# One matmul for a weight block's products with the high and low parts of 256 tokens, in two halves of a PSUM bank

## The chip, the cores and the metric

The kernel runs on one core of one Trainium2 chip. A time is the device time of one execution in microseconds (us); the one given for a kernel is the median of its runs. Before the change that is 3179.44 us in three runs (3178.3 to 3180.76).

## What is computed

Two transformer blocks, each of two layers, follow each other on 256 tokens of 1024 channels, all in float32:

```python
# first block, for each of 2 layers
x = x + 0.5 * swiglu_ffn(rms_norm(x, ffn1_norm[i]), ffn1_w_in[i], ffn1_w_out[i])   # D_FF = 2816
proj = rms_norm(x, mix_norm[i]) @ w_in[i]
rx, rgate, q, k, v, f_logit, ga, gb = jnp.split(proj, split_idx, axis=-1)
ya = (rg_lru(causal_dwconv(rx, ...), ...) * jax.nn.gelu(rgate)) @ w_rnn_out[i]
yb = forgetting_attention(q, k, v, f_logit, ...) @ w_attn_out[i]                   # 8 heads of 128
merged = jax.nn.sigmoid(ga + mb_a) * ya + jax.nn.sigmoid(gb + mb_b) * yb
x = x + merged @ w_o[i]
x = x + 0.5 * swiglu_ffn(rms_norm(x, ffn2_norm[i]), ffn2_w_in[i], ffn2_w_out[i])
gate = jax.nn.sigmoid(rms_norm(x, ple_norm[i]) @ ple_w_gate[i] + ple_b_gate[i])
x = x + gate * (p[i] @ ple_w_proj[i])
# second block: x and a context of 256 tokens; layer 0 FFN, conformer convolution, FFN;
# layer 1 FFN, windowed attention with 16 query and 4 key heads, projection, FFN
```

## The kernel before, in words

**Products.** A float32 product is made of rounded parts: weight w = wh + wl, input x = xh + xl, and y = wh·xh + wh·xl + wl·xh. TensorE (PE) makes three matmuls of a block of 128 x 128 weights, on lines 683, 684 and 685 (962 to 964 in the values units, where the weights move and the input stands). The weights come as *units*: 1024 rows by 256 columns, 8 blocks deep (`kc`) and 2 tiles wide (`t`), so 16 products. The output units of the last third of an FFN are 6 deep: 12 products.

**Streaming.** A unit's raw weights come in by SP's DMAs, into 4 slots. ACT rounds them to `wh` (`hi`, line 1316, one instruction for each tile), DVE subtracts to get `wl` (`lo`, line 1787). Both do this for unit u + 2 while PE works on u: there are two buffers by parity. A unit's two tiles lie in two banks of PSUM, again by parity. Each engine's program is written out by hand, in order; semaphores link them: `mm_done` (a tile's products are there), `hi_done`, `lo_done`, `banks_free` (DVE or ACT has read the banks).

**Order of stages.** Layer of the first block, all at 256 tokens: FFN1, the mixer, FFN2, the PLE gate. An FFN goes in three groups: gate-and-up units (G), then four output units (O), whose result is added to x. The mixer goes through units for gates, the recurrence's input, queries and keys, then four *values units* (V0 to V3), four units of the merge gate (GB), four output units of the recurrence (RNN), four of the attention (ATT) and four of the output projection (WO). The heads are spread over them: from V3 on, step st does, between the two tiles of a unit and behind it, scores of head st (line 1000), turning head st - 1's probabilities (line 972) and its values. The second block mostly works on x and context together, 512 tokens at once; only its query units (K2_Q), output projection (K2_WO) and last FFN (K2_FFN4) are at 256.

**Norms that are put off.** Behind FFN1, the mixer and FFN2 of the first block, the next stage's first units work on x before its norm. For that, ACT and DVE do the following for each of the last four output units i. ACT: both `hi` of unit u + 2, squares of x (line 1352, `Tt`), x times the gain rounded (line 1360, `Fh` or `Hh`); for i = 3 a table load comes between the `hi`, and the squares stand ahead of the second. DVE: `lo` of tile 0, the low part of x for i - 1, the update of x (line 1967 through the helper on line 1779), `lo` of tile 1. PE sums the squares (line 723) ahead of block 4 of the next stage's first unit for the last, and spreads the roots (line 751) at block 7. `Fl` is the low part, `Rr` the roots.

**Readers of a unit's banks.** The x update is one instruction of 128 x 512 with factor 0.25; the values are copied by DVE (line 2202) to `Vb`; ACT takes the merge gate's tanh straight from the banks; RNN and ATT are multiplied by their gates in one instruction each; the queries of the second block are scaled by DVE (line 2523).

## Time and profile before

| what | value |
|---|---|
| median of three runs | 3179.44 us (3178.3 to 3180.76) |
| span of the profiled execution | 3176.8 us |
| PE busy | 3133.6 us, 99%, 21659 instructions |
| DVE busy | 2103.7 us, 66% |
| ACT busy | 1328.4 us, 42% |
| granted clock of PE | 9 tenths or more in each of the 40 slices |
| lines 683 to 685, x from `Fh`, `Fl` | 3296 products, 304 + 302 + 302 ns as the mean of one |

The profile is of one execution. Its span is 3176.8 us, about 2.6 us under the median of the runs, which holds what lies outside the span too. Matmuls overlap, so the mean duration of one is more than the time from one start to the next; the pitch is read from the timeline. A releaser in square brackets in a row is what ended the idle time before that instruction.

### The profile page before, as it was taken

To read this page: it belongs to the slowest core of one execution; us is meant where nothing else is said; L and a number is where in the kernel's file an instruction comes from. 1 tells how busy PE (TensorE), PEld (TensorE's weight loads), DVE (VectorE), ACT (ScalarE), POOL (GpSimd) and SP (SyncE) were. 2 spreads that over 40 slices of the span, in tenths; PEclk is the share of its full clock that TensorE was granted. 3 is DMA by queue.
4 is the path that set the end of the run, shared out by engine and by line. 5 is a ranking of instruction groups with operands and counts; after the bars stand their busy time and mean duration, and the time that the engine had idled before them with its cause. 6 is when DMAs were issued, how large, how long until landed. Compare 5 with 4: busy or idle time off the path is not lost.

```text
span 3176.8 us, 51940 instructions
## 1 busy us (share of the span) xinstructions
PE 3133.6 (99%) x21659; PEld 2775.9 (87%) x21659; DVE 2103.7 (66%) x3503; ACT 1328.4 (42%) x2009; POOL 2.3 (0%) x6
## 2 busy tenths in 40 slices
PE   8999999999999999999999999999999999999999
PEld 8999999999999999997888766788887888875999
DVE  6777756667677756657676487666646666464555
ACT  4455555455455554454232323422224222337444
POOL 0000000000000000000000000000000000000000
PEclk9999999999999999999999999999999999999999
DMA  7665446657655456665444454445435554340663
GB/s 207 186 172 175 152 137 181 181 185 205 183 172 171 139 161 175 179 224 147 146 133 139 134 145 135 141 125 159 133 108 148 154 147 124 116 146 1 188 184 107
DMA packets 682467, 488.05 MB, mean 154 GB/s; under 512 B 24575, under 2 KB 681337, under 8 KB 682233
## 3 DMA queue, kind: packets, MB, share of 16 engines
q1 hardware_dynamic: 677113, 480.21, 51.0%
q10 hardware_dynamic: 5120, 4.53, 0.6%
q8 instruction: 171, 2.80, 0.4%
q14 instruction: 63, 0.52, 0.1%
HBM read 474.57 MB, written 1.05 MB: 150 GB/s over the span
## 4 chain that ended last, share of the span: by engine, by line
PE 90%; DVE 4%; ACT 3%; DMA 1%; DVEq 1%; issue 1%; ACTq 0%; SPq 0%
PE ps L683 27%; PE ps L684 26%; PE ps L685 26%; DVE wl L1787 1%; PE ps L1144 1%; DVE Pp L1779 1%; PE ps L1269 1%; PE ps L1248 1%; ACT wh L1316 1%; DVE Hl L1779 1%; PE ps L1259 1%; PE ps L751 1%; PE ps L962 0%; PE ps L963 0%; PE ps L964 0%
## 5 line engine op out<-in xcount | busy, mean ns | idle before, releaser
L1787 DVE TENSOR_TENSOR wl<-raw,wh 128x1024 fp32r<-128x1024 f32 (+2 forms) x780 | 921.2, 1185 | 693.9 <-ACT wh L1316 692.0
L1316 ACT ACTIVATE wh<-raw 128x1024 fp32r<-128x1024 f32 (+2 forms) x780 | 794.1, 1026 | 1383.6 <-PE ps L685 1341.9
L683 PE MATMUL ps<-Fh,wh 128*128 128x256 f32 (+1 forms) x3296 | 1001.3, 304 | 6.3 <-DVE Fl L2458 3.0
L684 PE MATMUL ps<-Fl,wh 128*128 128x256 f32 (+1 forms) x3296 | 995.5, 302 | 0.0
L685 PE MATMUL ps<-Fh,wl 128*128 128x256 f32 (+1 forms) x3296 | 995.4, 302 | 0.0
L683 PE MATMUL ps<-Hh,wh 128*128 128x256 f32 (+1 forms) x2576 | 870.8, 338 | 6.9 <-DVE wl L1787 3.3
L684 PE MATMUL ps<-Hl,wh 128*128 128x256 f32 (+1 forms) x2576 | 856.6, 333 | 0.0
L685 PE MATMUL ps<-Hh,wl 128*128 128x256 f32 (+1 forms) x2576 | 856.4, 332 | 0.0
L683 PEld LDWEIGHTS ps<-Fh,wh 128*128 128x128 f32 x3296 | 629.7, 191 | 36.4 <-DVE Fl L2458 5.1
L685 PEld LDWEIGHTS ps<-Fh,wl 128*128 128x128 f32 x3296 | 629.8, 191 | 23.3
L684 PEld LDWEIGHTS ps<-Fl,wh 128*128 128x128 f32 x3296 | 629.9, 191 | 22.7
L683 PEld LDWEIGHTS ps<-Hh,wh 128*128 128x128 f32 x2576 | 488.7, 190 | 81.2 <-DVE Hl L1779 16.6
L685 PEld LDWEIGHTS ps<-Hh,wl 128*128 128x128 f32 x2576 | 488.9, 190 | 47.8
L684 PEld LDWEIGHTS ps<-Hl,wh 128*128 128x128 f32 x2576 | 489.0, 190 | 46.2 <-issue 1.0
L1779 DVE SCALAR_TENSOR_TENSOR QK<-raw,cs,QK 128x256 f32<-128x256 f32 x504 | 222.0, 482 | 17.9
L1445 ACT ACTIVATE Fh<-Pp 128x256 fp32r<-128x256 f32 (+1 forms) x176 | 85.9, 488 | 101.6 <-DVE Pp L1962 92.0
L1962 DVE TENSOR_TENSOR Pp<-Ss,ps 128x512 f32<-128x512 f32 (+1 forms) x88 | 54.7, 621 | 49.1 <-PE ps L685 43.9
L1779 DVE SCALAR_TENSOR_TENSOR Xx<-ps,G,Xx 128x256 f32<-128x256 f32 x112 | 52.3, 479 | 43.6 <-PE ps L685 41.2
L1932 DVE TENSOR_TENSOR Ss<-ps,Ss 128x256 f32<-128x256 f32 x88 | 37.4, 425 | 29.9 <-PE ps L685 20.9
L1405 ACT ACTIVATE Hh<-Pp,MOD 128x256 fp32r<-128x256 f32 x88 | 39.7, 501 | 40.1 <-DVE Pp L1779 40.1
L1983 DVE TENSOR_TENSOR Fl<-Pp,Fh 128x512 fp32r<-128x512 f32 (+1 forms) x88 | 54.4, 618 | 0.0
L1779 DVE SCALAR_TENSOR_TENSOR Ss<-Tt,ps 128x512 f32<-128x512 f32 (+1 forms) x88 | 54.1, 615 | 0.0
(307 smaller groups left out, 2204.8 us busy)
## 6 DMA issues: line engine op xcount, KB each, us to landing
raw<-in_ffn_w_in SPq DMA_DIRECT2D x176, 512.0 KB, 5.2
raw<-in_ffn_wi SPq DMA_DIRECT2D x176, 512.0 KB, 5.3
raw<-in_ada_w SPq DMA_DIRECT2D x144, 512.0 KB, 4.5
raw<-in_w_in SPq DMA_DIRECT2D x112, 512.0 KB, 4.6
raw<-in_ffn_w_out SPq DMA_DIRECT2D x64, 512.0 KB, 4.1
raw<-in_ffn_wo SPq DMA_DIRECT2D x64, 512.0 KB, 4.6
raw<-in_ffn_w_out SPq DMA_DIRECT2D x32, 384.0 KB, 3.8
raw<-in_ffn_wo SPq DMA_DIRECT2D x32, 384.0 KB, 3.8
```

Of the source, the lines that this page charges most:

```text
L683: nc.tensor.matmul(o, wh[:, u.par, kc, w], xh(kc), start=(kc == 0), stop=False)
L684: nc.tensor.matmul(o, wh[:, u.par, kc, w], xl(kc), start=False, stop=False)
L685: return nc.tensor.matmul(o, wl[:, u.par, kc, w], xh(kc), start=False, stop=(kc == kc_n - 1))
L751: mm = nc.tensor.matmul(ps[:, b, n // 4 * g:n // 4 * (g + 1)], one_row, Rr[:, 0:n // 4], start=True, stop=True)
L1316: nc.scalar.activation(tile_of(wh[:, u.par], t, n), tile_of(raw[:, u.slot], t, n), ACT.Copy) \
L1405: ins = nc.scalar.activation(Hh[:, s, kc, :], src, ACT.Identity, bias=shift(kc, s))
L1445: nc.scalar.activation(dst, src, ACT.Copy).then_inc(fh_done, 1)
L1779: return V.scalar_tensor_tensor(out=o, in0=in0, scalar=scalar, in1=in1, op0=op0, op1=op1)
L1787: V.tensor_tensor(tile_of(wl[:, u.par], t, n), tile_of(raw[:, u.slot], t, n), tile_of(wh[:, u.par], t, n).bitcast(F32), ALU.subtract).then ...
L1932: V.tensor_tensor(Ss[:, 0:n], bank(u, 0, n), r, ALU.mult).then_inc(a_done, 1)
L1962: V.tensor_tensor(Pp[:, u.par, 0:n], Ss[:, 0:n], bank(u, 1, n), ALU.mult) \
L1983: V.tensor_tensor(o, p, h.bitcast(F32), ALU.subtract).then_inc(f_done, 1)
```

## The change

The units with a 256-token input on the list (the FFN output units at 256 tokens, GB, RNN, ATT, WO, K2_Q, K2_WO) are computed with two matmuls for each product. The first takes `wh` and moves xh and xl together, 512 columns, into the two halves of a bank; the second takes `wl` and moves xh, 256 columns, into the first half. The high and low buffers become one array (`HH`, `FF`, `ww`) so that one operand reaches both. In the values units the input stands and [wh | wl] moves in one 512-column matmul, then wh with the low part of the input. In all, 1520 + 128 products. Whoever reads a bank now adds its halves:

- x updates: two instructions of DVE with a drain between, in place of one;
- values, ATT and the second block's queries: ACT copies the second half to SBUF (`spill_part`), then DVE adds the first to it (`add_first_part`), waiting on `spilt`;
- GB: DVE adds by a reduction (`add_parts`) in front of the scores' maxima, ACT's tanh follows on `gb_there`; RNN: `add_parts`, drain, then the product;
- the gated x update of the second block: four instructions and a drain in place of two.

```diff
-            def out_of(u, t, n):
-                return bank(u, t, n) if n == T else two(bank(u, t))
-
-            def linear(u, xh, xl, n, kc_n=C, ready=None, tiles=(0, 1), together=True, between={}):
+            def linear(u, x, n, kc_n=C, ready=None, tiles=(0, 1), together=True, between={}, halves=False):
 
 
                 def products(kc, t):
                     w = slice(P * t, P * t + P)
-                    o = out_of(u, t, n)
-                    nc.tensor.matmul(o, wh[:, u.par, kc, w], xh(kc), start=(kc == 0), stop=False)
-                    nc.tensor.matmul(o, wh[:, u.par, kc, w], xl(kc), start=False, stop=False)
-                    return nc.tensor.matmul(o, wl[:, u.par, kc, w], xh(kc), start=False, stop=(kc == kc_n - 1))
+                    whole, low = wh[:, u.par, kc, w], wl[:, u.par, kc, w]
+                    if halves:
+                        nc.tensor.matmul(two(bank(u, t)), whole, x(slice(0, 2), kc), start=(kc == 0), stop=False)
+                        return nc.tensor.matmul(bank(u, t, T), low, x(0, kc), start=False, stop=(kc == kc_n - 1))
+                    o = bank(u, t, T) if n == T else two(bank(u, t))
+                    nc.tensor.matmul(o, whole, x(0, kc), start=(kc == 0), stop=False)
+                    nc.tensor.matmul(o, whole, x(1, kc), start=False, stop=False)
+                    return nc.tensor.matmul(o, low, x(0, kc), start=False, stop=(kc == kc_n - 1))
 
...
-                            linear(u, part(Fh, n), part(Fl, n), n, held, ready if i == 0 else None)
+                            linear(u, part(FF, n), n, held, ready if i == 0 else None, halves=(n == T))
...
-                            o = bank(u, t, T)
-                            nc.tensor.matmul(o, Hh[:, 0, kc, tok], wh[:, u.par, kc, :], start=(kc == 0), stop=False)
-                            nc.tensor.matmul(o, Hl[:, 0, kc, tok], wh[:, u.par, kc, :], start=False, stop=False)
-                            mm = nc.tensor.matmul(o, Hh[:, 0, kc, tok], wl[:, u.par, kc, :], start=False,
+                            nc.tensor.matmul(two(bank(u, t)), Hh[:, 0, kc, tok], ww[:, :, u.par, kc, :], start=(kc == 0),
+                                             stop=False)
+                            mm = nc.tensor.matmul(bank(u, t, T), Hl[:, 0, kc, tok], wh[:, u.par, kc, :], start=False,
...
-                    linear(u, part(Hh, T), part(Hl, T), T, tiles=(0,))
+                    linear(u, part(HH, T), T, tiles=(0,), halves=True)
                     step_middle(1 + j)
-                    linear(u, part(Hh, T), part(Hl, T), T, tiles=(1,))
+                    linear(u, part(HH, T), T, tiles=(1,), halves=True)
...
+            def spill_part(o, u):
+
+                act.wait_ge(mm_done, u.mm_done(1))
+                _, b = parts(u)
+                nc.scalar.activation(o, b, ACT.Copy).then_inc(spilt, 1)
...
+                def summed_merge_gate(u, j):
+
+                    act.wait_ge(banks_free[u.par], u.read_out())
+                    for t in range(2):
+                        c = 2 * j + t
+                        nc.scalar.activation(Gb[:, c, :], Gb[:, c, :], ACT.Tanh, scale=0.5,
+                                             bias=half[:, R_MERGE + C + c:R_MERGE + C + c + 1]).then_inc(gb_there, 1)
...
+                def values_part(hp):
+                    spill_part(Vb[:, :, T * hp:T * (hp + 1)], Unit(k + M_V + hp))
+
                 stream(Unit(k + M_V))
+                values_part(0)
                 stream(Unit(k + M_V + 1))
+                values_part(1)
                 y_high(0)
                 stream(Unit(k + M_V + 2))
+                values_part(2)
 
...
                     hi(u.later(2), 0)
+                    if st == 0:
+                        values_part(3)
                     if st >= 2:
                         head_out(st - 2)
                     hi(u.later(2), 1)
                     if st >= 1:
                         copy_probs(st - 1)
                     if u.k < k + M_GB + 4 and st >= 1:
-                        merge_gate(u, Gb, st - 1, R_MERGE + C)
+                        summed_merge_gate(u, st - 1)
                     if st == 0:
                         y_high(1)
...
-                    stream(Unit(k + M_ATT + j))
+                    u = Unit(k + M_ATT + j)
+                    hi(u.later(2), 0)
+                    if j >= 2:
+                        act.wait_ge(m_done, l * 4 + (j - 1))
+                    spill_part(two(Pp[:, j % 2, :]), u)
+                    hi(u.later(2), 1)
                     act.wait_ge(mp_done, l * 4 + (j + 1))
                     nc.scalar.activation(Hh[:, 1, 2 * j:2 * j + 2, :], two(Pp[:, j % 2, :]), ACT.Copy) \
...
+            def add_parts(o, u):
+
+
+                return V.tensor_reduce(o, ps[:, 2 * u.par:2 * u.par + 2, :].rearrange("p t (h n) -> p t n h", h=2), AX_X, ALU.add)
+
+            def add_first_part(o, u, spills):
+
+                dve.wait_ge(spilt, spills)
+                return V.tensor_tensor(o, next(parts(u)), o, ALU.add)
...
-                            stt(x, pair(u), 0.25, x, ALU.mult, ALU.add).then_inc(banks_free[u.par], 1)
+                            a, b = parts(u)
+                            stt(x, a, 0.25, x, ALU.mult, ALU.add)
+                            dve.drain()
+                            stt(x, b, 0.25, x, ALU.mult, ALU.add).then_inc(banks_free[u.par], 1)
...
+                if n == T:
+                    for h in range(2):
+                        for t in range(2):
+                            x = Xx[:, 2 * i + t, :]
+                            ins = stt(x, ps[:, 2 * u.par + t, h * T:(h + 1) * T], gate(2 * i + t, 0), x, ALU.mult, ALU.add)
+                        if h == 0:
+                            dve.drain()
+                    ins.then_inc(banks_free[u.par], 1)
+                    return
...
-                    V.tensor_copy(Vb[:, :, T * hp:T * (hp + 1)], pair(u)).then_inc(banks_free[u.par], 1)
+                    add_first_part(Vb[:, :, T * hp:T * (hp + 1)], u, 8 * l + hp + 1).then_inc(banks_free[u.par], 1)
...
+                    if 1 <= st < 5:
+                        j = st - 1
+                        dve.wait_ge(mm_done, u.mm_done(1))
+                        add_parts(Gb[:, 2 * j:2 * j + 2, :], u).then_inc(banks_free[u.par], 1)
                     if st >= 5:
                         j = st - 5
                         dve.wait_ge(mm_done, u.mm_done(1))
                         ga = gateA[:, 2 * j:2 * j + 2, :]
-                        stt(ga, ga, 1.0, pair(u), ALU.add, ALU.mult).then_inc(banks_free[u.par], 1)
+                        add_parts(two(Pp[:, j % 2, :]), u).then_inc(banks_free[u.par], 1)
+                        dve.drain()
+                        stt(ga, ga, 1.0, two(Pp[:, j % 2, :]), ALU.add, ALU.mult)
...
-                    stt(two(Ss[:]), Gb[:, 2 * j:2 * j + 2, :], 1.0, pair(u), ALU.add, ALU.mult) \
-                        .then_inc(banks_free[u.par], 1)
+                    add_first_part(two(Pp[:, j % 2, :]), u, 8 * l + 5 + j).then_inc(banks_free[u.par], 1)
+                    dve.wait_ge(gb_there, (l * 4 + (j + 1)) * 2)
+                    dve.drain()
+                    stt(two(Ss[:]), Gb[:, 2 * j:2 * j + 2, :], 1.0, two(Pp[:, j % 2, :]), ALU.add, ALU.mult)
                     dve.drain()
...
-                V.tensor_scalar(Qb[:, 2 * j:2 * j + 2, :], pair(u), HD ** -0.5, None, ALU.mult) \
-                    .then_inc(banks_free[u.par], 1)
+                add_first_part(Qb[:, 2 * j:2 * j + 2, :], u, 8 * DEPTH + j + 1).then_inc(banks_free[u.par], 1)
```

On PE, in the last group of an FFN at 256 tokens; `Fh` and `Fl` are the input's parts, `wh` and `wl` the weights', line 723 sums the squares of x. Before:

```order
L683 MATMUL ps<-Fh,wh 128x256
L684 MATMUL ps<-Fl,wh 128x256
L685 MATMUL ps<-Fh,wl 128x256
L683 MATMUL ps<-Fh,wh 128x256
L684 MATMUL ps<-Fl,wh 128x256
L685 MATMUL ps<-Fh,wl 128x256
L723 MATMUL ps<-Tt,ones 32x64 x8
L683 MATMUL ps<-Fh,wh 128x256
L684 MATMUL ps<-Fl,wh 128x256
```

and of the changed kernel (`FF` holds both parts of the input, `ww` both of the weights, line 729 sums the squares):

```order
L686 MATMUL ps<-FF,ww 128x512
L687 MATMUL ps<-FF,ww 128x256
L686 MATMUL ps<-FF,ww 128x512
L687 MATMUL ps<-FF,ww 128x256
L729 MATMUL ps<-Tt,ones 32x64 x8
L686 MATMUL ps<-FF,ww 128x512
L687 MATMUL ps<-FF,ww 128x256
L686 MATMUL ps<-FF,ww 128x512
```

A product has three rows before and two now; the sums of squares stand where they stood.

On DVE at the end of FFN1 of layer 0, through to the root's reciprocal; `Xx` is x. Before:

```order
L1779 SCALAR_TENSOR_TENSOR Fl<-Xx,par,Fh 128x256 x2
L1779 SCALAR_TENSOR_TENSOR Xx<-ps,Xx 128x512
L1787 TENSOR_TENSOR wl<-raw,wh 128x6x128
L1787 TENSOR_TENSOR wl<-raw,wh 128x8x128
L1779 SCALAR_TENSOR_TENSOR Fl<-Xx,par,Fh 128x256 x2
L1779 SCALAR_TENSOR_TENSOR Xx<-ps,Xx 128x512
L1787 TENSOR_TENSOR wl<-raw,wh 128x8x128 x2
L1779 SCALAR_TENSOR_TENSOR Xx<-ps,Xx 128x512
L1779 SCALAR_TENSOR_TENSOR Fl<-Xx,par,Fh 128x256 x4
L1787 TENSOR_TENSOR wl<-raw,wh 128x8x128
L1826 RECIPROCAL Rr<-Rr 128x64
```

and of the changed kernel:

```order
L1811 SCALAR_TENSOR_TENSOR FF<-Xx,par,FF 128x256 x2
L1811 SCALAR_TENSOR_TENSOR Xx<-ps,Xx 128x512 x2
L1829 TENSOR_TENSOR ww<-raw,ww 128x6x128
L1829 TENSOR_TENSOR ww<-raw,ww 128x8x128
L1811 SCALAR_TENSOR_TENSOR FF<-Xx,par,FF 128x256 x2
L1811 SCALAR_TENSOR_TENSOR Xx<-ps,Xx 128x512 x2
L1829 TENSOR_TENSOR ww<-raw,ww 128x8x128 x2
L1811 SCALAR_TENSOR_TENSOR Xx<-ps,Xx 128x512 x2
L1811 SCALAR_TENSOR_TENSOR FF<-Xx,par,FF 128x256 x4
L1829 TENSOR_TENSOR ww<-raw,ww 128x8x128
L1868 RECIPROCAL Rr<-Rr 128x64
```

Each update of x (`Xx<-ps,Xx`) stands twice; nothing else has moved.

On ACT in the values units; `wh<-raw` rounds a tile of weights, `Fh<-Pp` a part of the recurrence's output. Before:

```order
L1328 ACT_TABLE_LOAD
L1328 ACTIVATE half<-half 128x1
L1316 ACTIVATE wh<-raw 128x8x128 x4
L1482 ACTIVATE Fh<-Pp 128x512
L1316 ACTIVATE wh<-raw 128x8x128 x4
L1482 ACTIVATE Fh<-Pp 128x512
```

and of the changed kernel:

```order
L1337 ACT_TABLE_LOAD
L1337 ACTIVATE half<-half 128x1
L1319 ACTIVATE ww<-raw 128x8x128 x2
L1326 ACTIVATE Vb<-ps 128x2x256
L1319 ACTIVATE ww<-raw 128x8x128 x2
L1326 ACTIVATE Vb<-ps 128x2x256
L1491 ACTIVATE FF<-Pp 128x512
L1319 ACTIVATE ww<-raw 128x8x128 x2
L1326 ACTIVATE Vb<-ps 128x2x256
L1319 ACTIVATE ww<-raw 128x8x128
L1326 ACTIVATE Vb<-ps 128x2x256
L1319 ACTIVATE ww<-raw 128x8x128
```

The copies `Vb<-ps` are new; each waits for its unit's last matmul, and stands behind the two roundings of unit u + 2. The one of V3 stands between two roundings.

## Rows read from the trace of the kernel before

**Rows 1.** the page's part 4, the chain that ended last, by engine
```profile
PE 90%; DVE 4%; ACT 3%; DMA 1%; DVEq 1%; issue 1%; ACTq 0%; SPq 0%
```

**Rows 2.** PE's timeline (start us, us, engine, line, operation), 256-column matmuls, FFN1
```profile
199.87 0.28 PE L683 MATMUL ps<-Fh,wh 128*128 128x256 f32 x1
...
205.51 0.28 PE L685 MATMUL ps<-Fh,wl 128*128 128x256 f32 x1
```

**Rows 3.** PE's timeline, 512-column matmuls of the second block
```profile
1600.24 0.39 PE L683 MATMUL ps<-Hh,wh 128*128 128x512 f32 x1
...
1615.20 0.39 PE L683 MATMUL ps<-Hh,wh 128*128 128x512 f32 x1
```

**Rows 4.** DVE's timeline, first output unit of attention, layer 0
```profile
451.05 0.68 DVE L1779 SCALAR_TENSOR_TENSOR Ss<-Gb,ps 128x512 f32<-128x512 f32 x1
451.82 0.69 DVE L1779 SCALAR_TENSOR_TENSOR Pp<-Ss,gateA 128x512 f32<-128x512 f32 x1
452.43 1.22 DVE L1787 TENSOR_TENSOR wl<-raw,wh 128x1024 fp32r<-128x1024 f32 x1
```

**Rows 5.** ACT's timeline, last three output units of FFN1, layer 0
```profile
208.26 0.63 ACT L1352 ACTIVATE Tt<-Xx 128x512 f32<-128x512 f32 x1 [1.59 <-DVE Xx L1779]
...
213.33 0.63 ACT L1352 ACTIVATE Tt<-Xx 128x512 f32<-128x512 f32 x1 [1.58 <-DVE Xx L1779]
...
217.60 0.63 ACT L1352 ACTIVATE Tt<-Xx 128x512 f32<-128x512 f32 x1 [0.38 <-DVE Xx L1779]
```

**Rows 6.** PE's timeline, first norm behind FFN1, layer 0
```profile
218.85 0.43 PE L723 MATMUL ps<-Tt,ones 128*32 128x64 f32 x16
...
221.75 1.10 PE L751 MATMUL ps<-Rr,co 128*128 128x64 f32 x8
...
230.09 0.36 PE L683 MATMUL ps<-Fh,wh 128*128 128x256 f32 x1 [0.70 <-DVE Tt L2161]
```

**Rows 7.** ACT's timeline, square roots and values units, layer 0
```profile
346.33 0.60 ACT L1551 ACTIVATE Tt<-ps 128x512 f32<-128x512 f32 x1 [1.15 <-PE ps L685]
...
358.67 2.01 ACT L1316 ACTIVATE wh<-raw 128x1024 fp32r<-128x1024 f32 x2 [3.17 <-PE ps L964]
...
365.41 1.99 ACT L1316 ACTIVATE wh<-raw 128x1024 fp32r<-128x1024 f32 x2
```

**Rows 8.** DVE's timeline, values units, layer 0
```profile
359.76 2.36 DVE L1787 TENSOR_TENSOR wl<-raw,wh 128x1024 fp32r<-128x1024 f32 x2 [0.46 <-ACT wh L1316]
...
366.48 2.36 DVE L1787 TENSOR_TENSOR wl<-raw,wh 128x1024 fp32r<-128x1024 f32 x2 [1.04 <-ACT wh L1316]
...
368.76 0.68 DVE L2250 TENSOR_TENSOR QK<-QK,ps 128x512 f32<-128x512 f32 x1
```

**Rows 9.** PE's timeline, scores of head 0 and turning its probabilities
```profile
370.38 0.39 PE L1000 MATMUL ps<-QK 128*128 128x128 f32 x2
...
378.56 0.49 PE L972 MATMUL ps<-co,Tt 128*128 128x128 f32 x3
```

**Rows 10.** ACT's timeline, probabilities of head 0
```profile
377.11 0.80 ACT L1582 ACTIVATE Tt<-Tt,tiny 128x128 f32<-128x128 f32 x2 [0.28 <-DVE tiny L2279]
```

**Rows 11.** DVE, the reductions of line 2545 (ns min/median/max)
```profile
L2545 DVE TENSOR_REDUCE tiny<-ps x16: 1224/1225/1225, 2852.9 to 2925.6; 128x2 f32<-128x1024 f32 x16
```

**Rows 12.** ACT's timeline, output projection of the mixer, layer 0
```profile
474.81 0.63 ACT L1352 ACTIVATE Tt<-Xx 128x512 f32<-128x512 f32 x1 [0.95 <-DVE Xx L1779]
```

**Rows 13.** PE's timeline, spread of the roots behind the mixer, layer 0
```profile
496.43 1.00 PE L751 MATMUL ps<-Rr,co 128*128 128x64 f32 x8
```

**Rows 14.** ACT's timeline, last output unit of FFN2, layer 0
```profile
681.85 0.63 ACT L1352 ACTIVATE Tt<-Xx 128x512 f32<-128x512 f32 x1 [1.58 <-DVE Xx L1779]
...
685.00 0.62 ACT L1352 ACTIVATE Tt<-Xx 128x512 f32<-128x512 f32 x1
```

**Rows 15.** PE's timeline, first unit of the gate behind FFN2
```profile
687.38 0.43 PE L723 MATMUL ps<-Tt,ones 128*32 128x64 f32 x16
```

**Rows 16.** DVE's timeline, last query unit of the second block
```profile
2845.42 0.69 DVE L2523 TENSOR_SCALAR QK<-ps 128x512 f32<-128x512 f32 x1 [0.50 <-PE ps L685]
```

More of the change, by code:

```diff
@@ L417, in pair, with parts @@
             return ps[:, 2 * u.par:2 * u.par + 2, 0:T]
+        def parts(u):
+            return (ps[:, 2 * u.par:2 * u.par + 2, h * T:(h + 1) * T] for h in range(2))
         def two(ap):
@@ L457, in unscaled @@
         def unscaled(norm):
-            return (Hh, Hl) if norm % 4 == 3 else (Fh, Fl)
+            return HH if norm % 4 == 3 else FF
         def inverse_root(norm):
@@ L1073, in _ @@
                 for j in range(4):
-                    linear(Unit(k + M_ATT + j), part(Fh, T, 1), part(Fl, T, 1), T, ready=o_ready if j == 0 else None,
-                           between={3: last_values} if j == 0 else {})
+                    linear(Unit(k + M_ATT + j), part(FF, T, 1), T, ready=o_ready if j == 0 else None,
+                           between={3: last_values} if j == 0 else {}, halves=True)
                 def m_ready(kc):
@@ L1080, in _ @@
                 for j in range(4):
[L1081 removed]
+                    linear(Unit(k + M_WO + j), part(HH, T, 1), T, ready=m_ready if j == 0 else None, halves=True)
                     if j >= 1:
@@ L1292, in _ @@
             for j in range(4):
-                linear(Unit(K2_WO + j), part(Fh, T), part(Fl, T), T, ready=o2_ready if j == 0 else None)
+                linear(Unit(K2_WO + j), part(FF, T), T, ready=o2_ready if j == 0 else None, halves=True)
             norm_sums(14, T, K2_FFN4)
```

67 lines of the change are left out of this document (35 added, 32 removed).

## Prediction

> **What bounds the kernel now.** I began with the page's busy shares and the chain of work that ended last. PE is busy for 99% of the span and makes up 90% of that chain; DVE and ACT come to 7% [rows 1]. So one engine bounds nearly everything, and less work on PE should pay, except where PE already runs just behind a chain of DVE and ACT. To find those places I then read the timelines of PE, DVE and ACT around each group of units that the change touches.
>
> Next, what a matmul costs. In FFN1, 47 steps of 256 columns take 5.64 us: 120 ns each [rows 2]. 66 steps of 512 columns take 14.96 us: 226.7 ns each [rows 3]. The second 256 columns cost 106.7 ns, so some 13.2 ns of a matmul do not depend on its width. The change keeps 768 columns for each product and takes one matmul away: 3 x 119.9 - (226.7 + 119.9) = 13.2 ns.
>
> **The gain on PE.** 1648 products (1520 + 128) x 13.2 ns = 21.7 us: 0.21 us for a unit of 16 products, 0.16 for one of 12. No row shows a 512-column matmul alternating with one of 256. If the pair saved nothing, the gain would be 0; if the whole pitch of a matmul went it would be more, but the columns exclude that. I take 13.2, on the rows of either width.
>
> The Trainium skill, "TensorE: Matmul & The Clock Gate" (Part 2, and its section on the back-to-back issue gap), has a warm matmul start N / 2.4 GHz + about 2.5 ns behind the one before. By that a product would give back only 2.5 ns, 4.1 us in all, estimated from the page. The trace has 13 ns for these operands and decides; what remains of the rule is a rival below.
>
> **What is added, and where it stands.** The prices: a DVE instruction of 128 x 512 lets the next one start after 0.61 us, and with a drain between after 0.77 [rows 4]. The second instruction of an x update therefore costs 0.77. An ACT copy of 128 x 512 out of PSUM is 0.60 long (the square at 346.33 is of that shape) [rows 7]; I take 0.55, since neighbours overlap a little. The reduction over halves reads 128 x 1024, and the one of that size takes 1.22 [rows 11].
>
> "VectorE: DVE Perf Modes" of the Trainium skill ("The DRAIN you can't avoid") says that every DVE instruction is followed by a flush of its pipeline, so that a drain written out should cost nothing more. The trace has 0.77 against 0.61, so here it costs 0.16. By the page each x update would be 0.16 cheaper, some 2 us over the kernel.
>
> *Middle of the FFNs.* The output units of the first two groups, 8 for each FFN, have only DVE's x update behind them, which nobody awaits: DVE is busy 66%. The update's extra 0.77 lies beside 5.5 us of PE's work. Full gain: 8 x 0.21 = 1.69 us for each FFN.
>
> *End of FFN1.* Here the update is on a closed loop: squares (ACT), x times gain (ACT), `hi` (ACT), `lo` (DVE), low part (DVE), update (DVE), next squares. The squares start at 208.26, 213.33 and 217.60; from the first to the second are 5.07 us [rows 5], though PE needs about 4.8 for such a unit (12 products x 0.36 and the sums, 0.43 long [rows 6]). So the loop turns without slack, and its last turn still ends with DVE's update. 4 updates x 0.77 = 3.08 us later, less 0.16 since the first unit of the group ends earlier: +2.92. Behind it come the sums at 218.85 (1.25 after the last squares began), the root and its reciprocal, and the spread at 221.75, 4.15 after them; at 230.09 PE waits 0.70 for DVE in the same chain [rows 6]. PE cannot make it up. FFN1's last group: **+2.9**, not the -0.63 of the matmuls. At most 3.1; the other end is -0.6, if the loop had slack for all.
>
> *Values units and the first head.* PE's end of V1 releases ACT's two `hi` at 358.67 [rows 7]. That end comes 0.42 earlier now (V0 and V1). Then: `hi` 358.25 to 360.25, copy to 360.8, the add to 361.4, and only then `lo`, which stood at 359.76 [rows 8]. DVE is 1.64 late. The shift passes through the recurrence step to ACT's `Fh` and the next `hi` at 365.41 -> 367.05 [rows 7]. Both `hi` are done at 369.05, the copy of V2 at 369.6, its add at 370.2, `lo` x2 (2.28 from 366.48 to 368.76 [rows 8]) at 372.5, and the queries and keys of head 0 (368.76 before) 0.7 later, at 373.2. PE's scores of head 0 begin at 370.38 [rows 9], released by PE itself. They will wait for that instruction: **+2.9**. The first three GB units then give 0.63 back. Against it, head 0's probabilities are scaled at 377.11, over about 0.8, and PE turns them at 378.56 [rows 9, 10]: slack of 0.65. The next two turns have a reduction of 1.22 ahead of the maxima; behind a whole tile of products on PE they have more slack, which I estimate at nearly 2. I put 1.0 for the three (0 if slack covers all, 2.4 if both reductions count in full). Sum of the stage to the start of GB3: 2.9 - 0.63 + 1.0 = **+3.3**. The low end is -1.5 (seven units' gain, everything hidden), the high one +4.7.
>
> *GB3, RNN0 to RNN3, ATT0.* 6 units x 0.21 = **-1.27**. The 9 us step holds DVE's reductions (1.22, not on a turn).
>
> *ATT1 to ATT3, WO and the norm behind.* ATT1 to ATT3 and W0 give 0.84. The last low part for W0 comes later by the copy (0.55) and the add with its drain (0.77), 1.3; PE meets it at W0's seventh block, where I estimate a wait of 0.8 after some slack. Then the update: squares of the first WO unit at 474.81 [rows 12] become 475.5. From there the loop is the one of FFN1, 5.07 + 0.77 = 5.84 twice and 4.27 + 0.77 = 5.04: 492.3, and 4.15 on, the spread: 496.4. It stands at 496.43 now [rows 13]: the deeper units of WO left slack here. I take **+0.3** for ACT's order in it, 0 to 1.
>
> *End of FFN2.* The loop again: 3 x 0.77 - 0.16 brings the squares at 681.85 to 684.0. The last pass holds `hi` of a small unit, the table load and the squares, 3.15 us [rows 14]: 687.15 instead of 685.00. The sums, 1.25 behind the squares, would come at 688.4 instead of 687.38 [rows 15]: **+1.0** (0 to 2.2).
>
> One layer: -1.69 + 2.92 + 3.3 - 1.27 + 0.3 - 1.69 + 1.0 = +2.9; two layers **+5.7**.
>
> *Second block.* Queries: copy and add stand between PE and the rotation of the last tile, behind one `hi` (1.0 each in rows 7): 1.6 later than DVE's read at 2845.42 [rows 16], less 0.63 from three units (Q0's goes into a wait on the rotation): +1.0. Output projection: four units give 0.84, and its last update gets two more instructions of 128 x 256 and a drain, an estimated 0.98 (0.77 [rows 4] and 0.2 for being cut in two): +0.1. Last FFN: 8 x 0.21 + 4 x 0.16 = 2.32, less 0.98: -1.3. Together **-0.2**.
>
> **Sum.** +5.5 us: of 21.7 on PE some 12 are kept, and some 17 go into waits. The profiled execution was 3176.8, with 2.6 outside its span (3179.44 - 3176.8). 3176.8 + 5.5 + 2.6 = 3184.9, so **3185 us**, its own range 3181 to 3189.
>
> **Rivals.**
> 1. *The reduction over halves is dearer than its size (slower).* It reads a pair 256 elements apart for each of 512 results, where the row I price it by gives two results. At 2.2 us instead of 1.22 each of the turns 1 to 3 takes one more: +3 for a layer, 3191. For it: no row has this pattern. Against: 4-byte reads, the same count. It decides once the reduction passes about 1.9, where the turn's slack is gone.
> 2. *The waits are hidden and the gain stands (faster).* 3179.4 - 21.7 = 3158. For it: PE at 99%. Against: the squares' tight 5.07, and V2's copy behind two `hi`.
> 3. *The heads take up their part.* Copies and adds fit beside PE, only the x updates cost: per layer 3.3 becomes -1.5, and 5.5 becomes -4: 3175. Against it: the queries' instruction at 368.76 stands behind `lo` in DVE's order, whose `hi` stands behind ACT's copies.
> 4. *A matmul's fixed time isn't saved.* A 256-column matmul behind one of 512 may hide its weight load and still cost 133. With 2.5 ns a product kept, 81% of the 12 us kept goes: +9.5, 3194. This is also what the page's rule gives.
>
> That the change does not do what it says has no case of its own: the rows on PE are two for a product.
>
> **Chances.** What a measurement tells from no change is 0.2%, 6.4 us: same is 3173.1 to 3185.8. Forecast 0.62, rival 1 0.14, rival 2 0.05, rival 3 0.10, rival 4 0.05, anything else 0.04 (half of it faster). The forecast's band lies 0.36 in same and 0.26 in slower; rivals 1 and 4 are slower; 3 is same at 0.07 and faster at 0.03; 2 is faster. Faster 0.10, same 0.44, slower 0.46. The range for 8 in 10, 3173 to 3195, holds the forecast, rival 1 and most of 3 and 4.
>
> **What would show it.** PE: starts 347 ns apart from one product to the next; at 360 the fourth rival is right. ACT's squares at the end of FFN1 spaced 5.84, and the spread 2.9 later than 221.75. Scores of head 0 released by DVE's queries-and-keys instruction, not by PE. The reduction at 1.2. FFN1's output units in the middle 0.21 us shorter each, with no wait. I am wrong if the loop turns in less than 5.5, since then another instruction had slack in it, or if V2's `lo` does not wait for the copy.

## The result, and the profile of the changed kernel

The changed kernel takes 3198.02 us in the median of four runs (3197.03 to 3201.59), beside 3179.69 for the kernel before on the same chip. The ratio is 1.0060, 95% interval 1.0046 to 1.0075: slower by 0.6%, some 19 us. I had forecast 3185 (range 3173 to 3195), slower but by a third of that, and the time lies outside the range.

The head of the page and its chain, for the changed kernel:

```profile
span 3196.8 us, 48888 instructions
PE 3133.4 (98%) x20011; PEld 2691.9 (84%) x20011; DVE 2174.9 (68%) x3615; ACT 1336.4 (42%) x2029; POOL 2.3 (0%) x6
PE 85%; DVE 7%; ACT 4%; DVEq 2%; issue 1%; DMA 1%; ACTq 0%; SPq 0%
```

PE has 1648 instructions fewer, as intended, and is busy for the same time (3133.4 us, 3133.6 before). In the chain that ended last, DVE and ACT have gone from 7% to 11% [rows 1].

**What a product costs now.** PE's timeline of the changed kernel, in an output unit of FFN1 (columns as in [rows 2]):

```profile
196.17 0.40 PE L686 MATMUL ps<-FF,ww 128*128 128x512 f32 x1
196.40 0.28 PE L687 MATMUL ps<-FF,ww 128*128 128x256 f32 x1
196.52 0.40 PE L686 MATMUL ps<-FF,ww 128*128 128x512 f32 x1
...
202.18 0.40 PE L686 MATMUL ps<-FF,ww 128*128 128x512 f32 x1
```

From 196.17 to 202.18 are 17 products: 353.5 ns each. Three matmuls took 360.0 (three steps of [rows 2]). A product saves 6.5 ns by this stretch, half of the 13.2 that I put in.

**The end of FFN1.** ACT's squares of the four last output units, then PE's sums and the spread of the roots:

```profile
203.56 0.63 ACT L1361 ACTIVATE Tt<-Xx 128x512 f32<-128x512 f32 x1 [1.66 <-DVE Xx L1811]
208.91 0.63 ACT L1361 ACTIVATE Tt<-Xx 128x512 f32<-128x512 f32 x1 [2.46 <-DVE Xx L1811]
214.75 0.63 ACT L1361 ACTIVATE Tt<-Xx 128x512 f32<-128x512 f32 x1 [2.51 <-DVE Xx L1811]
219.79 0.63 ACT L1361 ACTIVATE Tt<-Xx 128x512 f32<-128x512 f32 x1 [1.14 <-DVE Xx L1811]
```

```profile
215.44 0.43 PE L729 MATMUL ps<-Tt,ones 128*32 128x64 f32 x16 [0.97 <-ACT Tt L1361]
220.47 0.43 PE L729 MATMUL ps<-Tt,ones 128*32 128x64 f32 x16 [1.43 <-ACT Tt L1361]
223.94 1.10 PE L757 MATMUL ps<-Rr,co 128*128 128x64 f32 x8 [0.69 <-DVE Rr L1868]
```

The loop turns in 5.84 us (208.91 to 214.75) and 5.04, both as forecast, where it turned in 5.07 and 4.27 [rows 5]. PE now waits for it three times; the spread is at 223.94, 2.2 later than in [rows 6], and PE had been 1.0 ahead of the kernel before.

**Values units and the first head.** ACT, DVE and PE of the changed kernel, layer 0:

```profile
360.51 2.01 ACT L1319 ACTIVATE ww<-raw 128x1024 fp32r<-128x1024 f32 x2 [2.38 <-PE ps L967]
362.43 0.58 ACT L1326 ACTIVATE Vb<-ps 128x512 f32<-128x512 f32 x1
368.81 0.63 ACT L1491 ACTIVATE FF<-Pp 128x512 fp32r<-128x512 f32 x1 [5.81 <-DVE Pp L2268]
369.35 1.99 ACT L1319 ACTIVATE ww<-raw 128x1024 fp32r<-128x1024 f32 x2
371.25 0.58 ACT L1326 ACTIVATE Vb<-ps 128x512 f32<-128x512 f32 x1
```

```profile
371.93 0.69 DVE L1821 TENSOR_TENSOR Vb<-ps,Vb 128x512 f32<-128x512 f32 x1 [3.15 <-ACT Vb L1326]
372.54 2.35 DVE L1829 TENSOR_TENSOR ww<-raw,ww 128x1024 fp32r<-128x1024 f32 x2
374.80 0.68 DVE L2304 TENSOR_TENSOR QK<-QK,ps 128x512 f32<-128x512 f32 x1
...
388.79 1.22 DVE L1816 TENSOR_REDUCE Gb<-ps 128x512 f32<-128x1024 f32 x1
```

```profile
361.25 0.50 PE L965 MATMUL ps<-ww,HH 128*128 128x512 f32 x1 [0.83 <-DVE ww L1829]
...
375.54 0.49 PE L1003 MATMUL ps<-QK 128*128 128x128 f32 x2 [2.31 <-DVE QK L2304]
```

The steps come in the order of the forecast: two roundings, copy, add, `lo` twice, queries and keys, and only then PE, which waits 2.31 us. One wait was not in the forecast: at 361.25 PE already waits 0.83 us for a `lo` of DVE, in either layer. The scores were at 370.38 [rows 9]; at that point PE is 5.2 us later than in the kernel before, 3.0 of it from the values units on. The reduction takes 1.22, as in [rows 11].

More that was not forecast stands behind the wait for head 0. Busy time of each engine in stretches of 10 us around the first head, layer 0 and layer 1, of the changed kernel; the third last column is PE's granted clock:

```profile
366.00:376.00 10.00, 7.69 (x46) 6.51 (x45) 6.70 (x10) 5.50 (x7) 0.00 (x0) 1.00 0.35 107
376.00:386.00 10.00, 10.00 (x52) 8.42 (x50) 8.54 (x15) 3.88 (x9) 0.00 (x0) 0.83 0.51 162
1073.00:1083.00 10.00, 7.68 (x47) 6.55 (x45) 6.70 (x10) 5.50 (x7) 0.00 (x0) 1.00 0.34 105
1083.00:1093.00 10.00, 10.00 (x41) 8.22 (x41) 8.64 (x15) 3.30 (x8) 0.00 (x0) 0.66 0.48 158
```

PE waits 2.3 us in both layers; after it the granted clock is 0.83 on average in one stretch and 0.66 in the other, that is 1.2 GHz for about 3.5 and 7 us, and 52 and 41 matmuls are done (the experiment busy10, below, does 56 and 55). By the same matmuls in both traces, PE goes from 5.16 to 6.5 us behind in layer 0 and from 11.5 to 14.2 in layer 1, while it does units that are shorter than before.

**Where the 20 us of the two profiled executions are** (3176.8 and 3196.8; how much later the same matmul starts, differences by stage):

| stage | forecast, a layer | layer 0 | layer 1 |
|---|---|---|---|
| FFN1, first two thirds | -1.7 | -1.0 | -1.0 |
| end of FFN1 to the spread | +2.9 | +3.2 | +3.2 |
| values units to head 0's scores | +2.9 | +3.0 | +3.0 |
| to the third turn (GB0 to GB2) | +0.4 | +1.3 | +2.7 |
| GB3 to the spread behind the mixer | -1.0 | -0.2 | 0.0 |
| FFN2, first two thirds | -1.7 | -0.9 | -0.9 |
| end of FFN2 | +1.0 | +1.2 | +1.4 |

That is 14.8 us at the end of the first block. The second adds 5.2: 1.8 in the queries and the attention behind them, with PE's wait of 1.57 us for the add of the last tile (forecast 1.6), 0.7 in the output projection, -0.2 in the last FFN, and 2.9 in the convolution, which the change does not touch. Nearly all of those 2.9 stand in one place. Rows of ACT's queue and of PE there in the kernel before:

```profile
1946.82 5.48 ACTq L1673 DMA_DIRECT2D shifted<-Vb  x8
1954.40 0.42 PE L723 MATMUL ps<-Gb,ones 128*32 128x128 f32 x8 [1.53 <-ACT Gb L1656]
1954.75 2.94 PE L672 MATMUL ps<-co 128*128 128x128 f32 x24
```

and in the changed kernel, with a stretch that shows its clock, 0.83:

```profile
1961.33 7.01 ACTq L1703 DMA_DIRECT2D shifted<-Vb  x8
1970.44 0.42 PE L729 MATMUL ps<-Gb,ones 128*32 128x128 f32 x8 [3.06 <-ACT Gb L1686]
1970.80 4.57 PE L677 MATMUL ps<-co 128*128 128x128 f32 x24
...
1965.00:1975.00 10.00, 6.94 (x87) 5.84 (x80) 3.98 (x7) 2.52 (x4) 0.00 (x0) 0.83 0.81 246
```

Eight DMA issues held ACT for 1.53 us longer, PE waited 1.53 us longer for it, and behind that wait the granted clock fell, so that the same 24 padding matmuls took 1.6 us more. Why the issues took longer is open: for the same group of eight the kernels of this study have 5.4 to 7.0 us. The experiment no_second, whose code is the same up to there, loses 0.3 us in this stretch and not 2.9. Over all kernels it moved by -0.5 to +3.5 us against the kernel before, so single profiles are compared up to the end of the first block only, and whole kernels by their medians.

### The profile page after: what moved, and what is told of

Same layout as the page of the kernel before. It is cut to its first block, busy times and chain, and to the rows that moved or that the text cites. A ratio compares the mean times of both kernels' runs of the same rounds, so it can differ in the third digit from the quotient of the medians.

```text
span 3196.8 us, 48888 instructions
## 1 busy us (share of the span) xinstructions
PE 3133.4 (98%) x20011; PEld 2691.9 (84%) x20011; DVE 2174.9 (68%) x3615; ACT 1336.4 (42%) x2029; POOL 2.3 (0%) x6
## 4 chain that ended last, share of the span: by engine, by line
PE 85%; DVE 7%; ACT 4%; DVEq 2%; issue 1%; DMA 1%; ACTq 0%; SPq 0%
PE ps L689 21%; PE ps L690 21%; PE ps L691 21%; PE ps L686 9%; PE ps L687 4%; DVE ww L1829 2%; ACT ww L1319 2%; DVE Pp L1811 1%; DVE Xx L1811 1%; PE ps L1272 1%; PE ps L1251 1%; PE ps L1147 1%; DVE HH L1811 1%; PE ps L1262 1%; PE ps L757 1%
## 5 line engine op out<-in xcount | busy, mean ns | idle before, releaser
L1829 DVE TENSOR_TENSOR ww<-raw,ww 128x1024 fp32r<-128x1024 f32 (+2 forms) x780 | 919.9, 1184 | 652.3 <-ACT ww L1319 650.5
L1319 ACT ACTIVATE ww<-raw 128x1024 fp32r<-128x1024 f32 (+2 forms) x780 | 793.5, 1026 | 1345.9 <-PE ps L691 1093.5
L689 PE MATMUL ps<-HH,ww 128*128 128x512 f32 (+1 forms) x2256 | 777.5, 345 | 6.9 <-DVE ww L1829 3.2
L690 PE MATMUL ps<-HH,ww 128*128 128x512 f32 (+1 forms) x2256 | 766.2, 340 | 0.0
L691 PE MATMUL ps<-HH,ww 128*128 128x512 f32 (+1 forms) x2256 | 766.0, 340 | 0.0
L689 PE MATMUL ps<-FF,ww 128*128 128x256 f32 (+1 forms) x2096 | 659.6, 315 | 6.3 <-DVE FF L2523 3.1
L690 PE MATMUL ps<-FF,ww 128*128 128x256 f32 (+1 forms) x2096 | 656.1, 313 | 0.0
L691 PE MATMUL ps<-FF,ww 128*128 128x256 f32 (+1 forms) x2096 | 656.0, 313 | 0.0
L689 PEld LDWEIGHTS ps<-HH,ww 128*128 128x128 f32 x2256 | 427.1, 189 | 79.0 <-DVE HH L1811 16.5
L691 PEld LDWEIGHTS ps<-HH,ww 128*128 128x128 f32 x2256 | 427.2, 189 | 47.7
L690 PEld LDWEIGHTS ps<-HH,ww 128*128 128x128 f32 x2256 | 427.4, 189 | 45.5
L686 PE MATMUL ps<-FF,ww 128*128 128x512 f32 x1200 | 428.1, 400 | 0.0
L689 PEld LDWEIGHTS ps<-FF,ww 128*128 128x128 f32 x2096 | 397.9, 190 | 34.7 <-DVE FF L2523 5.1
L691 PEld LDWEIGHTS ps<-FF,ww 128*128 128x128 f32 x2096 | 397.9, 190 | 23.3
L690 PEld LDWEIGHTS ps<-FF,ww 128*128 128x128 f32 x2096 | 398.0, 190 | 22.7
L687 PE MATMUL ps<-FF,ww 128*128 128x256 f32 x1200 | 337.0, 281 | 0.0
L686 PEld LDWEIGHTS ps<-FF,ww 128*128 128x128 f32 x1200 | 225.5, 188 | 56.3 <-issue 0.4
L687 PEld LDWEIGHTS ps<-FF,ww 128*128 128x128 f32 x1200 | 226.8, 189 | 0.0
L1454 ACT ACTIVATE FF<-Pp 128x256 fp32r<-128x256 f32 (+1 forms) x176 | 85.9, 488 | 101.9 <-DVE Pp L2004 92.1
L686 PE MATMUL ps<-HH,ww 128*128 128x512 f32 x320 | 120.5, 416 | 1.2 <-DVE HH L2355 1.2
```

The source lines that it names most:

```text
L686: nc.tensor.matmul(two(bank(u, t)), whole, x(slice(0, 2), kc), start=(kc == 0), stop=False)
L687: return nc.tensor.matmul(bank(u, t, T), low, x(0, kc), start=False, stop=(kc == kc_n - 1))
L689: nc.tensor.matmul(o, whole, x(0, kc), start=(kc == 0), stop=False)
L690: nc.tensor.matmul(o, whole, x(1, kc), start=False, stop=False)
L691: return nc.tensor.matmul(o, low, x(0, kc), start=False, stop=(kc == kc_n - 1))
L1319: nc.scalar.activation(tile_of(wh[:, u.par], t, n), tile_of(raw[:, u.slot], t, n), ACT.Copy) \
```

## The experiments

All times are medians of 5 to 11 executions in five rounds; a ratio is to the kernel before, run beside them, with its 95% interval. The kernel before had 3179.4 in the first group (mid_only, mid_sorted, no_values, busy20), 3180.6 in the second (copy_first, no_chain, no_second, mid_heads_sorted) and 3178.9 in the third (busy10, repaired). "Back" is the difference of a median to the changed kernel's 3198.02; in the second group, by the ratios, it would be 1 to 2 us more. The edits are shown shortened, with long conditions given by what they come to.

**mid_only.** Halves only where no one waits for the update of x; all other units have three matmuls a product again, and their results are read in one instruction (the merge gate's are copied by DVE first):

```diff
-                            linear(u, part(FF, n), n, held, ready if i == 0 else None, halves=(n == T))
+                            linear(u, part(FF, n), n, held, ready if i == 0 else None, halves=(n == T and g < 2))
```

> Two matmuls a product only in the output units of the first two thirds of the five FFNs at 256 tokens (40 units, 640 products); everything else has three again. Theory A, from the changed kernel's trace: a 512-column matmul followed by one of 256 takes 235.5 + 117.8 = 353.3 ns instead of 359.8, so a product saves 6.5 ns and nobody waits for the longer update of x: 640 x 6.5 = 4.2 us faster than before, about 3175.5. Rival B, my forecast's term: 13.2 ns, 8.4 us, about 3171. Rival C: DVE's second instruction for each update costs even here, no change or slower.

3175.85 us, ratio 0.9988 (0.9979 to 0.9997): 3.8 us faster by the ratio, near the 4.2 of theory A; the interval reaches to 6.7, short of B's 8.4, and leaves out C. Here and in mid_sorted the second block's output projection has three matmuls but is still read as two halves, the second of which holds no product; its time is that of the longer update. In the trace PE gains 0.87 us for each FFN (128 products), so 6.8 ns a product, and nothing behind it is late.

**mid_sorted.** The same units, all wide matmuls of a tile first:

```diff
+                        for kc in range(kc_n):
+                            nc.tensor.matmul(two(bank(u, t)), wh[:, u.par, kc, P * t:P * t + P], x(slice(0, 2), kc), ...)
+                        for kc in range(kc_n):
+                            mm = nc.tensor.matmul(bank(u, t, T), wl[:, u.par, kc, P * t:P * t + P], x(0, kc), ...)
```

> As mid_only, but PE does all 512-column matmuls of a tile first and then all of its 256-column ones. If the missing half of the saving comes from the change of width from one matmul to the next (theory A1), the pitches go back to 226.7 and 119.9 and another 640 x 6.7 = 4.2 us come: 3171. If it comes from reading both parts of the input or from writing both halves of a bank (A2), 512 columns keep 235 and the time is that of mid_only.

3175.43 us, ratio 0.9984 (0.9976 to 0.9993). The medians do not tell it from mid_only. The trace does. PE's rows of one tile in an FFN:

```profile
87.66 2.00 PE L712 MATMUL ps<-FF,ww 128*128 128x512 f32 x8
89.50 1.11 PE L715 MATMUL ps<-FF,ww 128*128 128x256 f32 x8
90.45 2.00 PE L712 MATMUL ps<-FF,ww 128*128 128x512 f32 x8
```

Eight products take 2.79 us here, 349 ns each. Each FFN gains 1.43 us, 11.2 ns a product, against 0.87 (the first FFN 0.7, as the granted clock is 0.83 between 20 and 30 us). Over all such tiles the means from start to start are 230.6 ns (512 columns) and 118.9 (256), against 236.2 and 117.0 in turns. So most of what was missing comes back with the order (A1). The order changes how often `wh` and `wl` alternate too, but in the kernel before they alternate at one width and every step is 120 ns, so the change of width is what is left. What stays is in the wide matmul, 230.6 against 226.7 [rows 3]; A2 may hold for those 4 ns, which no run takes apart. Its profiled execution lost the gain to 2.7 us in the convolution, between 1426 and 1901, of which 1.7 fall where the granted clock is down.

**no_values.** The values units as in the kernel before, with three matmuls a product and no copy on ACT:

```diff
-                    add_first_part(Vb[:, :, T * hp:T * (hp + 1)], u, 8 * l + hp + 1).then_inc(banks_free[u.par], 1)
+                    V.tensor_copy(Vb[:, :, T * hp:T * (hp + 1)], pair(u)).then_inc(banks_free[u.par], 1)
```

> The changed kernel with the values units as before (three matmuls, DVE copies their result). Theory: the copy and the add there make PE wait 2.3 us for head 0 in each layer, and the clock granted to PE falls to half for some microseconds behind that wait; without them 3.0 + 1.6 us in layer 0 and 3.0 + 2.9 us in layer 1 come back, less 0.8 for the products' saving: 9 to 10 us faster than the changed kernel, 3188 to 3189. Rival: the reductions in the merge gate's steps then make PE wait instead, and under 4 us come back (3194 or more).

3188.74 us, ratio 1.0031 (1.0021 to 1.0042): 9.3 us back, and the interval is clear of the changed kernel's. Behind the first block PE is 4.75 us late instead of 14.78. The granted clock is 1.00 in both layers' stretches. The reductions of the merge gate are still there and PE waits for none of them: rival 1 of the prediction and this rival fall.

**busy20 and busy10.** Padding in the wait:

```diff
+                    if st == 0:
+                        keep_busy(6, 20)   # busy10: 10
```

> The changed kernel with 20 matmuls of 128 x 128 on the identity before head 0's scores in each layer, where PE waits 2.3 us for DVE. They fill the wait and change nothing else. Theory: what follows the wait at half clock (3.5 us in layer 0, 7 us in layer 1) costs 1.6 + 2.9 us, and with PE busy the clock stays: 4 to 4.5 us faster than the changed kernel, about 3194. Rival: the clock falls for another reason (or its fall costs nothing), and the time stays at 3198.

3195.41 us, ratio 1.0052 (1.0039 to 1.0064): 2.6 us under the changed kernel's median, short of 4, and not told from it by the intervals. In the trace the clock stayed at 1.00, and PE lost nothing more behind the scores; but the scores themselves began 1.6 and 2.0 us later, since the padding took 4.5 us (the 20 matmuls show as 40 in the trace, the 10 of busy10 as 20).

> As busy20 with 10 padding matmuls: the profile of busy20 shows that each goes twice through the array, 20 took 4.5 us and put head 0's scores off by 1.6 to 2.0 us a layer, while the clock stayed. Ten take 2.2 us, which is the wait. Theory: nothing is put off now, and what the clock costs comes back in full, 1.8 + 3.1 us: 4.5 us faster than the changed kernel, 3193.5, and scores of head 0 where the changed kernel has them. Rival: 2.2 us of padding ends too early or too late and the clock falls all the same: 3198.

3194.93 us, ratio 1.0048 (1.0035 to 1.0060). PE's padding, the scores and the turn of the first head, then the same stretches as above, for busy10:

```profile
372.67 2.39 PE L677 MATMUL ps<-co 128*128 128x128 f32 x20
375.24 0.49 PE L1003 MATMUL ps<-QK 128*128 128x128 f32 x2 [0.17 <-DVE QK L2306]
...
383.80 0.52 PE L975 MATMUL ps<-co,Tt 128*128 128x128 f32 x3 [0.28 <-ACT Tt L1607]
```

```profile
366.00:376.00 10.00, 9.82 (x66) 8.75 (x64) 6.71 (x10) 5.50 (x7) 0.00 (x0) 1.00 0.36 110
376.00:386.00 10.00, 9.72 (x56) 7.88 (x55) 8.54 (x15) 4.62 (x10) 0.00 (x0) 1.00 0.52 172
1073.00:1083.00 10.00, 9.91 (x66) 8.81 (x65) 6.71 (x10) 5.50 (x7) 0.00 (x0) 1.00 0.39 116
1083.00:1093.00 10.00, 9.74 (x55) 7.94 (x55) 8.54 (x15) 4.62 (x10) 0.00 (x0) 1.00 0.51 172
```

The scores start at the same point as in the changed kernel, the wait is 0.17 instead of 2.31, the clock is 1.00 throughout, and by the third turn PE has lost 0.3 us in either layer instead of 1.3 and 2.7. At the end of the first block it is 3.2 us better than the changed kernel (11.62 against 14.78; 0.3 of it is there from the first matmuls on), and the median is 3.1 better. The two intervals overlap, but none of its five executions (up to 3195.35) is as slow as the fastest of the changed kernel's four (3197.03). Work that computes nothing kept the clock up in both layers and made the kernel faster: the clock is shown. Its price is nearer 3 than the 4.5 that I expected; with the clock up the turn itself waits 0.28 us for ACT, which takes part of it.

**copy_first.** ACT's copy ahead of the roundings, for V0 as shown, for V1 and V2 in the same way:

```diff
-                stream(Unit(k + M_V))
                 values_part(0)
+                stream(Unit(k + M_V))
```

> The changed kernel with ACT's copy of a values unit's second half put ahead of the two weight roundings (V0 to V2), not behind them. Theory: it is the copy's place in ACT's queue that makes DVE 1.6 to 3.7 us late for head 0, not the copy itself (0.58); now DVE is late by about 0.6, head 0's scores don't wait for it, and the clock doesn't fall behind them. 3.0 + 1.4 us in layer 0 and 3.0 + 2.7 in layer 1 come back: about 3188. Rival: the added instruction of DVE and the copy cost as such, the roundings now come later by as much as they were early, and the time stays within 2 us of 3198.

3187.83 us, ratio 1.0023 (1.0014 to 1.0033): 10.2 us back, with every product still in two matmuls. ACT, DVE and PE of copy_first, layer 0:

```profile
360.44 0.60 ACT L1326 ACTIVATE Vb<-ps 128x512 f32<-128x512 f32 x1 [2.31 <-PE ps L967]
360.93 2.00 ACT L1319 ACTIVATE ww<-raw 128x1024 fp32r<-128x1024 f32 x2
365.98 0.60 ACT L1326 ACTIVATE Vb<-ps 128x512 f32<-128x512 f32 x1 [3.05 <-PE ps L967]
```

```profile
361.14 0.69 DVE L1821 TENSOR_TENSOR Vb<-ps,Vb 128x512 f32<-128x512 f32 x1 [1.57 <-ACT Vb L1326]
362.01 2.36 DVE L1829 TENSOR_TENSOR ww<-raw,ww 128x1024 fp32r<-128x1024 f32 x2 [0.19 <-ACT ww L1319]
...
371.02 0.68 DVE L2304 TENSOR_TENSOR QK<-QK,ps 128x512 f32<-128x512 f32 x1
```

```profile
371.85 0.39 PE L1003 MATMUL ps<-QK 128*128 128x128 f32 x2
```

The add of V1 comes at 361.14, not 363.10; queries and keys at 371.02, not 374.80; the scores, at 371.85, wait for nobody, and neither does V2; the granted clock is 1.00 in both layers' stretches. The copy still takes 0.6 us, off the path; its place, with the clock that fell behind the wait, cost ten.

**no_chain.** Three matmuls in the last four output units of FFN1, FFN2 and in the mixer's projection:

```diff
+                            if g < 2:
                                 a, b = parts(u)
...
+                            else:
+                                stt(x, pair(u), 0.25, x, ALU.mult, ALU.add).then_inc(banks_free[u.par], 1)
```

> The changed kernel with three matmuls a product in the last four output units of FFN1 and FFN2 in the first block and in the mixer's output projection, whose updates of x are one instruction again. Theory: the loop of ACT and DVE turns at 5.07 us again, and 3.2 (FFN1), 0.4 (mixer) and 1.2 us (FFN2) come back in each layer: 9.5 us, about 3188.5. Rival: the waits of the values units take these up (they come later in the same layer, in a chain of their own), and under 5 us come back.

3188.55 us, ratio 1.0025 (1.0013 to 1.0036): 9.5 us back, the forecast number. The squares at the end of FFN1 start at 207.88, 212.94 and 217.21 again: 5.06 and 4.27 apart. The ends of FFN1 and FFN2 no longer lose anything; the mixer's projection gives nothing of the 0.4 expected (0.4 us worse in layer 0 from the third turn to the spread, the same in layer 1), so that the sum was met to 0.1 us by luck. The scores still wait (2.44 us in layer 0), and PE is 3.0 us later at them in both layers, so the two chains are independent.

**no_second.** Queries, output projection and last third of the last FFN of the second block with three matmuls:

```diff
-                linear(Unit(K2_Q + j), part(HH, T), T, halves=True)
+                linear(Unit(K2_Q + j), part(HH, T), T)
...
-                linear(Unit(K2_WO + j), part(FF, T), T, ready=o2_ready if j == 0 else None, halves=True)
+                linear(Unit(K2_WO + j), part(FF, T), T, ready=o2_ready if j == 0 else None)
```

> The changed kernel with three matmuls a product in the second block's queries, its output projection and the last third of its last FFN. Theory: the copy and the add before the rotation (1.8 us), and the longer gated updates at two stage ends (0.7 and 0.9 us) go, less 0.8 of saved products: 2.5 us faster, about 3195.5. Rival: that stage's tail waits for other work, and nothing can be told from 3198.

3194.71 us, ratio 1.0045 (1.0032 to 1.0057): 3.3 us back, where 2.5 were expected; the two intervals overlap widely, so the size is not shown well. In its trace PE loses nothing from 1963 on (14.68 to 13.11 us behind), where the changed kernel goes from 17.67 to 19.96. Part of that difference, some 1.5 us, can be the clock in the attention: it is down for about 7 us here and for about 10 in the changed kernel, and kernels whose code is the same there have either (7 in busy10, 10 in copy_first).

**mid_heads_sorted and repaired.** The kernel that the experiments point to: halves in the middle of the FFNs, the merge gate and the recurrence, sorted by width; then (repaired) the values units too, with the copy first. For the tiles of the merge gate and the recurrence, beside the edits of mid_sorted:

```diff
-                if halves and len(tiles) == 2 and not between:
+                if halves and not between:
```

> Two matmuls a product where nobody waits for the added work: the output units of the first two thirds of each FFN at 256 tokens, the merge gate's and the recurrence's output units; in each tile all 512-column matmuls first, then all 256-column ones. Everything else has three. From the pitches of the sorted order (231 + 119 against 360): 11 ns x (640 + 256) products = 10 us faster than before, about 3169.5. Rival: the reductions (1.22 each) make the heads' turns late, and the time is that of the sorted middle alone, 3172 to 3175.

3171.82 us, ratio 0.9974 (0.9964 to 0.9983): by the ratio 8 us faster than the kernel before and some 26 faster than the change. That lies between the theory's 10 and the sorted middle alone (5 by its ratio); the interval takes in the first and overlaps that of mid_sorted. The trace decides for the theory: the units of the merge gate and the recurrence gain 1.27 us in each layer, 10 ns a product, and no turn is late. PE's chain share is 90% again. The gain grows steadily through the first block to 7.5 us, and no stage of it gives any back; the profiled execution then loses 2.8 us in the convolution.

> mid_heads_sorted with two matmuls a product in the values units too, the copy ahead of the weight roundings as in copy_first. Theory: nobody waits for it, and 128 products x 6.5 ns = 0.8 us come on top: 3171.0, which can hardly be told from mid_heads_sorted (3171.8). Rival: without the other delays around it, the copy makes head 0's scores wait, and it is 2 us or more slower (3174).

3173.84 us, ratio 0.9983 (0.9974 to 0.9992): not told apart from mid_heads_sorted by these runs. In the traces its values units gain 0.7 us in each layer, more than the 0.4 expected, and the heads' steps up to the norm behind the mixer then gain 0.5 in place of 1.3: nothing is left of it. PE now waits 0.27 us for ACT at the first turn. Neither theory is right; no wait of 2 us came, and no net gain. mid_heads_sorted is the version to keep, as the simpler of two that are not told apart.

## Why the prediction was wrong

The direction was right and so were most of the waits; the sum was not: +5.5 forecast, +18 to +20 measured.

- **The step that failed** is the first term, "13.2 ns for a product": I took the pitch of each width from stretches of that width alone and added them, and named the alternation as unseen. In turns, the pair costs 353 ns, not 346.6, and a product gives back 6.5 to 6.8 ns. The prediction says that 12 us of gain are kept and 17 lost in waits; its own terms come to 15 kept (11.2 in the first block, 3.8 in the second) and 20.5 lost, which is the same +5.5. Half of the 15 was not there: about 7.5 us of the miss. My rival 4 had the direction (+9.5) and its reason, a 256-column matmul that costs 133, was wrong: the narrow one is cheap (117), the wide one dear (236). The Trainium skill's 2.5 ns ("TensorE: Matmul & The Clock Gate", Part 2) would make, as an estimate, a saving of 4.1 us in all; the trace has 6.5 to 6.8 ns in turns and 11.2 sorted, between its figure and mine.
- **The granted clock was missing**, a term that I put at nothing. I had the delay at head 0's scores (2.9 against 3.0) and priced only the wait. Behind it PE ran at 1.2 GHz for 3.5 and 7 us; busy10 shows this worth some 3 us of the 18. The kernel before keeps 1.00 there, but its own rows would have told me that a gap can cost the clock. Around waits of PE of 0.38 and 1.80 us in the attention it has

```profile
2850.00:2860.00 10.00, 7.98 (x45) 5.23 (x43) 7.95 (x22) 2.76 (x7) 0.00 (x0) 0.93 0.22 77
2860.00:2870.00 10.00, 9.83 (x28) 5.25 (x28) 3.63 (x12) 5.27 (x15) 0.00 (x0) 0.56 0.00 0
```

  (the granted clock stands third from the right). The source hints at it too: `keep_busy` (line 669) issues padding matmuls at 16 places of the kernel, and at none ahead of head 0's scores, where PE had no wait until the change made one.
- **The end of FFN1**: forecast +2.9, measured +3.2. Right, by no_chain. The drain costs 0.16 as in [rows 4]: the loop's 5.84 is 5.07 + 0.77.
- **Values units**: +2.9 against +3.0. The path was right, copy_first shows it; that the number fits to 0.1 us is in part luck. PE's wait of 0.83 us for V2's `lo` was not in it, and the gain of the products, which was, came to half. For the turns behind it I had 1.0 us for the reductions; in no_values, at full clock, the three units give 0.2 us of the 0.3 that their products are worth, so the reductions cost 0.1 at most, and the loss there is the clock.
- **Mixer's end, FFN2's end**: GB3 to the spread was forecast at -1.0 and came to -0.2 and 0.0, the product's term again for the most part; the end of FFN2 at +1.0 came to +1.2 and +1.4.
- **Second block**: forecast -0.2; the units that the change touches lose 2.3 us in the profile, and no_second puts them at 3.3, with a wide interval. The wait of the last query tile was right (1.6 against 1.57); most of the difference, 1.9 us, is the products' gain again. The 2.9 us in the convolution belong to the one profile.

Of the 14.5 us between the forecast's +5.5 and the profiles' +20.0, 7.5 are products and 2.9 the convolution. The turns' row adds 2.6 beside its products: there the clock costs more, and the reductions less, than the 1.0 a layer that I had. What is left, about 1.5 us, lies in small differences over the other rows and has no experiment of its own. The convolution's 2.9 are those of one execution, but the median of the four is only 0.5 below it, so the others are likely to lose about as much somewhere; no trace shows where.

The profiles differ by 20.0 us and the medians by 18.3. A span is 1.7 to 2.0 us under the time of its own execution wherever both are on record, so of the 2.6 us that I added for what lies outside the span, 0.8 belong to a profiled execution of the kernel before that was quicker than its median.

## What to carry to other kernels

Saving a matmul's fixed time is worth it only where PE itself is the last to be ready; each reader that gets one instruction more must be looked at by its own loop, and a copy that someone waits for belongs ahead of work that is not yet needed. A pitch is taken from the mix of shapes that will run, not from each shape alone. And a wait that a change puts on PE can cost more than its length: ask what the clock does behind it, and look whether the kernel already pads its waits.
